# A gated delta rule layer on one core: the chunk inverses in 64 by 64 blocks, and the rounds written out

## The reference

```
decay = where(causal, exp(g_i - g_j), 0)
a_low = where(strict, (k_beta @ k.T) * decay, 0)
w = triangular_solve(a_low + I, k_beta * exp(g), unit_diagonal)
u = triangular_solve(a_low + I, v_beta, unit_diagonal)
step: v_new = u - w @ S;  o = q_dec @ S + attn @ v_new
      S = S * exp(g_last) + k_dec.T @ v_new
```

## Time and profile before

| | us |
|---|---|
| median of 3 runs | 1267.94 |
| lowest, highest | 1267.55, 1269.01 |
| the profiled execution | 1267.8 |
| its span, first to last instruction | 1266.0 |

### The profile page before, as it was taken

How to read it: one execution, slowest core, us unless ns; L and a number is a source line. 1 busy time by engine, 2 the same in 40 slices (tenths; PEclk the granted TensorE clock), 3 DMA queues, 4 the chain that set the end, 5 groups by cost and what they waited for, 6 DMA issues and landing times.

```text
span 1266.0 us, 17440 instructions
## 1 busy us (share of the span) xinstructions
PE 1225.5 (97%) x6188; PEld 1024.7 (81%) x6188; DVE 826.8 (65%) x1261; ACT 470.7 (37%) x776; POOL 410.7 (32%) x371
## 2 busy tenths in 40 slices
PE   6999999999899999899999999999999999999998
PEld 6888777887788888888778888888888887888887
DVE  5546878786566666634675666565566579677776
ACT  5221322441343343323553333333333344344342
POOL 6001111342112222201664656675575456100000
PEclk9998999999899999999999999999999999999999
DMA  7411343535822221032414665653667349584544
GB/s 232 124 43 34 87 130 108 163 126 158 258 86 69 72 62 50 1 126 91 133 51 150 211 208 170 210 202 118 196 233 265 108 144 311 181 261 144 175 126 174
DMA packets 190886, 183.17 MB, mean 145 GB/s; under 512 B 19598, under 2 KB 146908, under 8 KB 190812
## 3 DMA queue, kind: packets, MB, share of 16 engines
q1 hardware_dynamic: 190688, 182.16, 45.4%
q10 hardware_dynamic: 124, 0.04, 0.0%
HBM read 124.50 MB, written 56.62 MB: 143 GB/s over the span
## 4 chain that ended last, share of the span: by engine, by line
PE 77%; DVE 11%; issue 4%; ACT 3%; POOL 3%; DMA 2%; ACTq 0%; SPq 0%; DVEq 0%; POOLq 0%
PE ps L2355 30%; PE ps L2360 14%; PE ps L2002 11%; PE ps L2126 5%; PE ps L2266 5%; PE ps L2233 2%; PE ps L2202 2%; PE ps L2221 1%; PE ps L1980 1%; DVE stage L1593 1%; DVE wop_lo L1872 1%; POOL mla_sc L963 1%; DVE xop L1856 1%; DVE row_stat L1804 1%; PE ps L2131 1%
## 5 line engine op out<-in xcount | busy, mean ns | idle before, releaser
L2355 PE MATMUL ps<-xop,wop_hi 128*128 128x512 f32 x1232 | 379.8, 390 | 1.7 <-DVE wop_lo L1872 1.0
L2355 PEld LDWEIGHTS ps<-xop,wop_hi 128*128 128x128 f32 x1232 | 230.8, 188 | 51.0 <-issue 2.3
L2355 PE MATMUL ps<-xop,wop_lo 128*128 128x512 f32 x616 | 239.7, 389 | 0.0
L2360 PE MATMUL ps<-dop,wop_hi 128*128 128x512 f32 x440 | 136.1, 390 | 2.3 <-DVE x L1954 2.2
L2355 PEld LDWEIGHTS ps<-xop,wop_lo 128*128 128x128 f32 x616 | 115.6, 188 | 24.2
L1872 DVE TENSOR_TENSOR wop_lo<-w_sumS,wop_hi 128x512 fp32r<-128x512 f32 (+1 forms) x104 | 88.8, 856 | 67.0 <-ACT wop_hi L1351 67.0
L1872 DVE TENSOR_TENSOR wop_lo<-w_pair,wop_hi 128x512 fp32r<-128x512 f32 (+1 forms) x76 | 86.0, 1133 | 36.1 <-ACT wop_hi L1351 36.0
L2002 PE MATMUL ps<-act_hi,w_hi 128*128 128x512 f32 x320 | 104.2, 407 | 0.2 <-DVE stage L1593 0.2
L1954 DVE TENSOR_TENSOR x<-x,ps 128x512 f32<-128x512 f32 x112 | 76.5, 683 | 37.2 <-PE ps L2360 37.2
L2002 PE MATMUL ps<-act_lo,w_hi 128*128 128x512 f32 x320 | 99.6, 393 | 0.0
L2360 PEld LDWEIGHTS ps<-dop,wop_hi 128*128 128x128 f32 x440 | 82.1, 188 | 21.5 <-DVE wop_lo L1872 3.0
(11 more groups left out here) (315 smaller groups left out, 2288.3 us busy)
## 6 DMA issues: line engine op xcount, KB each, us to landing
w_pair<-in_w_gate_up SPq DMA_DIRECT2D x44, 512.0 KB, 5.3
hidden<-up SPq DMA_DIRECT2D x22, 512.0 KB, 3.0
wd_rows<-in_w_down SPq DMA_DIRECT2D x22, 512.0 KB, 5.4
raw<-in_w_in SPq DMA_DIRECT2D x21, 512.0 KB, 4.3
wd_raw<-down_sums SPq DMA_DIRECT2D x12, 768.0 KB, 8.5
down_sums<-wd_rows SPq DMA_DIRECT2D x33, 256.0 KB, 2.6
wd_raw<-in_w_down SPq DMA_DIRECT2D x9, 768.0 KB, 7.4
qkv_kept<-qkv_st SPq DMA_DIRECT2D x12, 512.0 KB, 5.3
```

Of the source, the lines that this page charges most:

```text
L2355: last = pe.matmul(ps[:, bank, :].rearrange("p (t n) -> p t n", n=P), w[:, k, :], a[:, k, :, :], start=(p in ("P1", "P2", "P7") and k == 0 ...
L2360: last = pe.matmul(ps[:, bank, :], w[:, k, :], a[:, k, :], start=(p in ("P1", "P2", "P7") and k == 0 and w is wop_hi[s] and a is hi), stop ...
```

## The change

N is no longer doubled as a square of 128 by 128. Its two blocks of 64 by 64 are loaded side by side, into `N0`: 128 partitions, 64 columns per head, and `inverse_kept` in DRAM has half the columns. At the first level m0, x1 and y1 work on each block by itself, in two products of 64 by 64 by 64 per head, one from partitions 0 to 63 to output partitions 0 to 63 and one from 64 to 127 to 64 to 127. m0 is now a product with the identity. z1 is left out; a new stage m1 transposes the first block of the new N instead. At the second level x2 and y2 make only the corner that is new, and A is used itself, so that GpSimd's second mask product is left out. VectorE writes N block by block, and the lower left corner is cleared once, at the entry, behind the wait for the copy out of `pz`, which SP no longer makes. N0 is loaded when qs is done. There are 15 stages instead of 14. All `Fori` loops of the rounds are written out.

```diff
-LEVELS = [32, 64]
+LEVELS = [32]
+BLOCK = 64
...
+    base = Region(R1 + 176 * KB)
+    N0 = [base.take(f"N0_{b}", [P, 4, BLOCK]) for b in range(2)]
...
-        GDN_STAGES = ["pre", "qk", "turn", "m0", "x1", "yz1", "x2", "yz2", "ks", "tr", "av", "oms", "on", "ot"]
-        gp = [Steps(sem(f"gdn_pe{b}"), ["qk", "norms", "kT", "vT", "m0", "x1", "y1", "z1", "x2", "y2",
+        GDN_STAGES = ["pre", "qk", "turn", "m0", "x1", "y1", "m1", "x2", "y2", "ks", "tr", "av", "oms", "on", "ot"]
+        gp = [Steps(sem(f"gdn_pe{b}"), ["qk", "norms", "kT", "vT", "m0", "x1", "y1", "m1", "x2", "y2",
                                         "ks", "qs", "tr", "av", "ds", "ot"], ahead=True) for b in range(2)]
-        ga = [Steps(sem(f"gdn_act{b}"), ["sq", "m0", "x1", "x2", "osq"], ahead=True) for b in range(2)]
-        gd = [Steps(sem(f"gdn_dve{b}"), ["et", "att", "ss", "kd", "vn", "rqs", "r2", "n1", "m1", "n2", "r0", "r", "o1",
...
+        PAIR = [slice(0, BLOCK), slice(BLOCK, P)]
+
+        def blocks_view(bank, rows_p=slice(0, P)):
+            return ps[rows_p, bank, 0:4 * BLOCK].rearrange("p (h n) -> p h n", h=4)
+
+        M0 = [M_[b][:, 0:2, :].rearrange("p a (c n) -> p (a c) n", n=BLOCK) for b in range(2)]
+        M1 = [M_[b][0:BLOCK, 2:4, :].rearrange("p a (c n) -> p (a c) n", n=BLOCK) for b in range(2)]
+        X1 = [qkvf[b][:, 8:10, :].rearrange("p a (c n) -> p (a c) n", n=BLOCK) for b in range(2)]
+        X2 = [qkvf[b][BLOCK:P, 10:12, :].rearrange("p a (c n) -> p (a c) n", n=BLOCK) for b in range(2)]
...
-                    for c in range(TT):
-                        sp.dma_start(n_d[:, c, :, :], zeros[:, :, :]).then_inc(zeros_kept, 16)
+                    for c in range(0, TT, 2):
+                        sp.dma_start(n_d[:, c:c + 2, :, :].rearrange("p c h n -> p (c h n)"),
+                                     zeros[:, :, :].rearrange("p h n -> p (h n)")).then_inc(zeros_kept, 16)
...
                 at = ds(i * 2 + b, 1)
+                sp.dma_start(N0[b][:, :, :], n_d[:, at, :, :].rearrange("p a h n -> p (a h) n")).then_inc(n_loaded[b], 16)
                 sp.wait_ge(gp[b].sem, gp[b].after("tr", i - 1))
                 sp.dma_start(E_[b][:, :, :], e_d[at, :, :, :].rearrange("a p h n -> p (a h) n")).then_inc(e_loaded[b], 16)
-                sp.dma_start(N_[b][:, 0, :, :], n_d[:, at, :, :].rearrange("p a h n -> p (a h) n")).then_inc(n_loaded[b], 16)
...
-                sp.dma_start(n_d[rows_q, :, :, rows_q].rearrange("i c h j -> (c h) i j"),
+                in_block = slice(q % 2 * BASE, (q % 2 + 1) * BASE)
+                sp.dma_start(n_d[rows_q, :, :, in_block].rearrange("i c h j -> (c h) i j"),
                              n_base[rows_q, :, :]).then_inc(n_kept, 16)
             sp.wait_ge(n_kept, 16 * P // BASE)
-            sp.wait_ge(pool_moved, 2 * 16)
             for b in range(2):
-                sp.dma_start(N_[b][:, 0, :, :], n_d[:, b, :, :]).then_inc(n_loaded[b], 16)
+                sp.dma_start(N0[b][:, :, :], n_d[:, b, :, :]).then_inc(n_loaded[b], 16)
             for half in range(2):
                 for k in range(half * 4, half * 4 + 4):
                     sp.dma_start(w_out_sb[:, k, :], w_out[0, k * P:(k + 1) * P, :]).then_inc(w_out_loaded, 16)
-            with sp.Fori(1, TT // 2) as i:
+            for i in range(1, TT // 2):
...
-                    elif stage_name in ("m0", "x1"):
-                        l = 0 if stage_name == "m0" else 1
-                        if l == 0:
-                            pool.wait_ge(a_loaded[b], i * 16 + 16)
-                            pool.wait_ge(gd[b].sem, gd[b].after("o", i - 1))
-                        else:
-                            pool.wait_ge(gp[b].sem, gp[b].after("x1", i))
-                        pool.tensor_tensor(B_[b][:, :, :], A_[b][:, :, :], heads_of(masks[:, l, :]),
+                    elif stage_name == "m0":
+                        pool.wait_ge(a_loaded[b], i * 16 + 16)
+                        pool.wait_ge(gd[b].sem, gd[b].after("o", i - 1))
+                        pool.tensor_tensor(B_[b][:, :, :], A_[b][:, :, :], heads_of(masks[:, 0, :]),
...
-                        gsig(b, act.activation(flat(M_[b]), ps[:, W[b], :], ACT.Copy))
-                    elif stage_name in ("x1", "x2"):
-                        gafter(gp[b], stage_name)
-                        gsig(b, act.activation(qkvf[b][:, 8:12, :].rearrange("p h n -> p (h n)"), ps[:, U[b], :],
-                                               ACT.Copy))
+                        gsig(b, act.activation(M0[b], blocks_view(W[b]), ACT.Copy))
+                    elif stage_name == "x1":
+                        gafter(gp[b], "x1")
+                        gsig(b, act.activation(X1[b], blocks_view(U[b]), ACT.Copy))
+                    elif stage_name == "m1":
+                        gafter(gp[b], "m1")
+                        gsig(b, act.activation(M1[b], blocks_view(U[b], PAIR[0]), ACT.Copy))
+                    elif stage_name == "x2":
+                        gafter(gp[b], "x2")
+                        gsig(b, act.activation(X2[b], blocks_view(U[b], PAIR[1]), ACT.Copy))
...
             link(dve.memset(S_[:, :, :], 0.0))
+            dve.wait_ge(pool_moved, 2 * 16)
+            for b in range(2):
+                dve.memset(N_[b][BLOCK:P, 0, :, 0:BLOCK], 0.0)
...
-                    elif stage_name == "yz1":
+                    elif stage_name == "y1":
                         gafter(gp[b], "y1")
-                        gsig(dve.tensor_tensor(n_[:, 1, :, :], n_[:, 0, :, :], bank_w, ALU.subtract))
-                        gafter(gp[b], "z1")
-                        gsig(dve.tensor_tensor(m_[:, :, :], m_[:, :, :], bank_u, ALU.subtract))
-                    elif stage_name == "yz2":
+                        for rows_p in PAIR:
+                            op = dve.tensor_tensor(n_[rows_p, 0, :, rows_p], N0[b][rows_p, :, :], blocks_view(W[b], rows_p),
+                                                   ALU.subtract)
+                        gsig(op)
+                    elif stage_name == "y2":
                         gafter(gp[b], "y2")
-                        gsig(dve.tensor_tensor(n_[:, 0, :, :], n_[:, 1, :, :], bank_w, ALU.subtract))
+                        gsig(dve.tensor_scalar(n_[0:BLOCK, 0, :, BLOCK:P], blocks_view(W[b], PAIR[0]), -1.0, None, ALU.mult))
...
+                        def corner(bank, rows_p, h):
+                            return ps[rows_p, bank, h * BLOCK:(h + 1) * BLOCK]
...
-                        four_t(W[b], n_(0), cnt)
+                        for h in range(4):
+                            for rows_p in PAIR:
+                                last = pe.matmul(corner(W[b], rows_p, h), N0[b][rows_p, h, :], ident[rows_p, rows_p],
+                                                 start=True, stop=True)
+                        last.then_inc(cnt.sem, 1)
                     elif stage_name == "x1":
                         gafter(gg[b], "b0")
                         gafter(ga[b], "m0")
                         gafter(gd[b], "vn")
-                        four(U[b], on(B_[b]), on(M_[b]), cnt)
-                    elif stage_name == "yz1":
+                        for h in range(4):
+                            for rows_p in PAIR:
+                                last = pe.matmul(corner(U[b], rows_p, h), B_[b][rows_p, h, rows_p], M0[b][rows_p, h, :],
+                                                 start=True, stop=True)
+                        last.then_inc(cnt.sem, 1)
+                    elif stage_name == "y1":
                         gafter(ga[b], "x1")
-                        four(W[b], x1, n_(0), cnt)
-                        four(U[b], n_(0), x1, cnt)
+                        for h in range(4):
+                            for rows_p in PAIR:
+                                last = pe.matmul(corner(W[b], rows_p, h), X1[b][rows_p, h, :], N0[b][rows_p, h, :],
+                                                 start=True, stop=True)
+                        last.then_inc(cnt.sem, 1)
+                    elif stage_name == "m1":
+                        gafter(gd[b], "n1")
+                        for h in range(4):
+                            last = pe.transpose(corner(U[b], PAIR[0], h), N_[b][0:BLOCK, 0, h, 0:BLOCK], ident[0:BLOCK, 0:BLOCK])
+                        last.then_inc(cnt.sem, 1)
                     elif stage_name == "x2":
-                        gafter(gg[b], "b1")
-                        gafter(gd[b], "m1")
-                        four(U[b], on(B_[b]), on(M_[b]), cnt)
-                    elif stage_name == "yz2":
+                        gafter(ga[b], "m1")
+                        for h in range(4):
+                            last = pe.matmul(corner(U[b], PAIR[1], h), A_[b][0:BLOCK, h, BLOCK:P], M1[b][:, h, :], start=True, stop=True)
+                        last.then_inc(cnt.sem, 1)
+                    elif stage_name == "y2":
                         gafter(ga[b], "x2")
```

(8 more changed lines are left out.)

12 lines of the change are left out of this document (7 added, 5 removed).

## The result

| | before | after |
|---|---|---|
| median, us | 1268.2 | 1282.0 |
| lowest, highest | 1267.6, 1269.0 | 1280.7, 1284.3 |
| span of the profiled execution | 1266.0 | 1279.8 |

The changed kernel is slower: ratio 1.0109, interval 1.0096 to 1.0122. I had forecast 1272.5, slower, in a range of 1265 to 1280. The direction was right, the size was three times too small, and the reason for it is one that my sum had nearly left out.

A forecast was written before the change was run, and what follows sets the result against it. TensorE, busy 97% of the span, was taken as the bound: passes plus standstills. Passes and waits -1.7, changes of shape +2.4, entry +4.6, clock -0.7 made +4.6 us: 1272.5, range 1265 to 1280.

The forecast's parts named there:

- the clock: At the entry: a second low-clock dip, 1.4 us dear, may stay out; half of it taken, -0.7 us.
- A: Chunk inverses in the rounds: 68 passes at 0.057 us replace 44 at 0.111, 8.1 us less for eight chunks.
- C: Rounds: 96 switches between full and 64 by 64 passes, 0.05 us each, half inside waits, +2.4 us, bounds 0 and 20.
- rival 1: Small-pass bursts: the two halves overlap and changes of shape are free; 1265 us, chance 0.16.
- B, the waits: TensorE's standstills in the rounds: some go, others appear; plus 1.6 us a round, 6.4 in four rounds.
- D, the entry: Before the rounds: VectorE waits for the pool copies, first row minimum 5.5 us later; +4.6 us net.
- The wait for N: At the entry: m0's 0.88 us wait for N to land goes, since N now has time.
- E: GpSimd's mask product, shorter copies, halved N load and written-out loops: priced at nothing.
- Rival 2: Each change of shape in the rounds empties the array, 0.22 us, +10.5 instead of 2.4; 1280.5 us, chance 0.17.

The follow-up runs named there:

- cured_w: cured with the first quarter of w_out split one step later in the first round; 1262.9 us, ratio 0.9952.
- fill_small: The changed kernel with fourteen unused 64 by 64 transposes ahead of the transpose of scores 1 in each round; 1275.0 us, ratio 1.0055.
- before_wait: The kernel before with VectorE waiting for the pool copies right after clearing S, nothing else changed; 1273.7 us, ratio 1.0035.
- halves_apart: The changed kernel with m0, x1 and y1 sending all upper-partition products first, then the lower ones, instead of alternating; 1292.5 us, ratio 1.0174.
- before_flat: The kernel before with its five loops over the rounds written out, nothing else; 1268.2 us, ratio 0.9994.
- cured: The changed kernel in its own order, corners cleared at the first write of N, unused full passes in four standstills of a round; 1270.6 us, ratio 1.0012.
- late_clear: The changed kernel with VectorE's wait for the pool copies and the corner clearing moved to the first write of N; 1277.5 us, ratio 1.0066.
- pe_order: late_clear with TensorE's own order changed in the rounds, no work added or left out; 1274.2 us, ratio 1.0039.
- before_idle: The kernel before, rounds written out, with four unused ScalarE copies ahead of the exponential of scores 3; 1271.6 us, ratio 1.0018.
- small_stream: The kernel before, rounds written out, with 64 unused 64 by 64 transposes ahead of the products of scores 7 each round; 1278.4 us, ratio 1.0078.

## Why the prediction was wrong

**The step that failed is the clock.** It stood in the sum with -0.7 us, as a matter of the entry alone; half clock inside the rounds had no term. What the runs show, by the profiled run of after: half clock takes about 11.1 us. That is 53.86 us for a first round that takes 49.5 in cured_w, and 51.88 and 52.39 for rounds that take 48.75. The first of these is an estimate across kernels; fill_small, with the entry of after, had a first round of 48.55 at a clock of 0.87, so it isn't too high. Besides, the entry costs 5.3 (before_wait: 4 to 5), and a round at full clock saves 1.5, in the three stretches behind the first 4.4. 5.3 - 4.4 + 11.1 and the 1.2 behind the rounds are 13.2 of 13.8.

Without its clock term my forecast was 1273.2. 1282.0 less 11.1 is 1270.9, so the rest of the sum was 2.3 us too high, and it came that near by errors that cancel, as the terms below show.

The trace that I argued from has the pattern. Weight loads of before at the entry:

```profile
324.20 0.97 PEld L2126 LDWEIGHTS ps<-qkvf 128*128 128x128 f32 x8 [2.58 <-DMA qkvf<-qkv_kept]
```

TensorE fell to half clock behind these 2.58 us, and stayed up behind 1.46 in the rounds. I took this for a matter of the entry and didn't ask how near the rounds come to it. My rule that an added wait costs its length was wrong by a factor here: the two rounds in which the clock fell behind the 1.09 us ahead of the transposes of scores 1, forecast at 1.3, took 3.1 and 3.6 us more than one at full clock. The upper end of my range rested on changes of shape and had no term for this at all. The period was to be 50.0 to 50.8 us; it was 48.75 at full clock and 51.88 where the clock fell, and never what I had said.

**A and C, passes and changes of shape.** Both were mis-sized, and they nearly cancelled. A pass of 64 by 64 in one half takes 0.058 us (eight loads in 0.54, less the last one's 0.135, in seven steps), against 0.057 forecast, and two halves side by side 0.027 a pass, which was my rival 1: a group of 16 took 0.54 us, its 0.5 and not my 0.9. Into a burst from full passes the first start comes 0.26 us behind the last one (395.82 to 396.08, instead of 0.11), and out of it 0.20 (the last small start is at 396.49, the next full at 396.69). That is 0.15 and 0.09 over a stream, 0.24 for the pair, where I had 0.10. Per chunk, from the last full start to the next full one, three bursts of 16 take 0.87, two of 8 about 0.9 and m1 about 0.65, each less the 0.11 of an ordinary step: 4.4 us, against 4.9 before. So A and C together gave 0.4 to 0.5 us a chunk, some -3.5 to -4 us in eight, not -5.7. The Trainium skill's sentence that changing the mode needs a drain ("TensorEngine Tiling (Array Packing)", Key Properties) agrees with the trace, at 0.24 us for both ways; its rule that tiles in different row groups run side by side ("TensorE: Matmul & The Clock Gate", Part 3) agrees too, with 0.027 against 0.058, and halves_apart shows that alternating them is what brings it.

**B, the waits,** was right in its places. Forecast gone and gone: those ahead of scores 4 and 2. Forecast and there: scores 1 (1.3 forecast, 1.09 found), m1 (0.4, 0.34), scores 5 (0.5, 0.44). Not there: tr and x2 (0.6 forecast, 0.17). And scores 3 went from 1.46 to 1.04. Together they are 5.1 to 5.3 us a round, as before, where I had added 1.6. But part of that is the loops: written out, the kernel before has only 4.5 us of waits, so the change added 0.6 to 0.8 us a round, half of my term. By these terms a round should be 0.1 to 0.4 us shorter than in before_flat; it is 0.7 shorter, and the rest isn't accounted for.

**D, the entry,** was right in its mechanism and place: 330.10 for a forecast 330.3, and 5.3 us for 5.5. The wait for N went, as forecast.

**E** was right by the median and wrong inside the rounds: writing them out shortens each by 0.8 us, which is half of the 1.5 that a round of after saves, and I had argued that there was nothing to gain. What I had not seen is that ScalarE holds M1 behind the load of w_out once the clearing is off the entry, 3.1 us of standstill and half clock from 348.0 to 361.7 in cured.

One number was misread: the weight loads of the earlier trace rows are busy 43.95 us, not 43.2. Nothing in the sum used it.

**The rivals.** Rival 2 gave 1280.5, near the measured time, and that is luck: a change of shape costs 0.12 us, half of its 0.22, and it has no word of the clock. Rival 1's mechanism was there, but its gain went into the changes of shape.

What isn't settled is when exactly the clock falls. 2.06 us between full passes lowered it in two of three rounds and 1.46 in none. 1.09 us, with 0.34 and small bursts beside it, lowered it in two of the four rounds of after, in all four of late_clear and in three of four of pe_order (1.08). In fill_small it fell once behind 0.34 and 0.21 us with small bursts. So standstill is enough by itself, and whether small passes beside it count for less than full ones is open.

## What to carry to other kernels

Where TensorE runs nearly all the time, read the granted clock of each stretch beside the standstills, not only their sum: here a wait of 1 to 2 us cost 1.5 to 3.6 more by the half clock behind it. Look for the longest standstill of a repeating list and break it up, first by the order of TensorE's own instructions, then, if nothing useful is at hand, by passes that nobody reads. Here an order took 0.8% off with full products, an order with filling as much with small ones, and doing one step that waits for a load later took 0.3% more. Full and small products then end at the same 1254.7 us: the small products' gain against the kernel before, at most 0.5% in cured_w, is not a gain over a better order.

Small products save TensorE time only in long bursts, with the two halves alternating: each burst costs 0.24 us for its way in and out, which is two full f32 passes.

## What the runs showed of the hardware that I had not expected

- Unused passes can make a kernel faster: nine in each round took 7 us off (1282.0 to 1275.2), and twenty in each round of pe_order took some 15 us off (1274.2 to 1258.4).
- Two 64 by 64 passes on different halves start 6 to 7 ns apart (after, from 396.084 us on), 0.027 us a pass on average; the same passes sent half by half take 0.046.
- TensorE kept its full clock through 3.60 us of nothing but 64 by 64 passes and lost it behind 2.06 us of standstill between full ones (before_idle). Short standstills mixed with small bursts lost it once too (fill_small).
- Half clock shows in each row as it is: eight 64 by 64 loads 0.54 us and 0.93 us, sixteen full ones of ks 1.87 us in small_stream, and eight of kd 1.83 us in before_idle.
